# Gated DeltaNet scan in a hybrid encoder step: two 64-row inverses and a substitution in place of one 128-row inverse, in another order of work

## What is computed

```python
# gated delta rule; l tokens in a chunk; kb = k*beta
a_mat = where(strict, einsum('nbhid,nbhjd->nbhij', kb, kc) * decay, 0)
rhs = concatenate([vc * bc, kb * exp(gcum)], -1)
sol = triangular_solve(a_mat + eye(l), rhs, lower=True, unit_diagonal=True)
u, w = sol[..., :dv], sol[..., dv:]
qk = where(causal, einsum('nbhid,nbhjd->nbhij', qc, kc) * decay, 0)
def step(s, xs):                       # scan over the chunks
    v_new = u_i - w_i @ s
    o = (q_i * exp(g_i)) @ s + qk_i @ v_new
    s = s * exp(g_last) + (k_i * exp(g_last - g_i)).T @ v_new
```

## Time and profile before

| | |
|---|---|
| median of three runs | 1979.21 us (1976.8 to 1980.09) |
| profiled execution | 1982.12 us |
| its span, first to last instruction | 1980.4 us |
| PE, busy share of the span | 92% |
| PE weight loads | 87% |
| DVE, ACT, POOL | 41%, 26%, 31% |
| mean granted TensorE clock | 0.956 of full speed |
| chain that ended last, by engine | PE 75%, DVE 14%, ACT 4%, issue 4% |

### The profile page before, as it was taken

One profiled execution on the slowest core, in us unless ns is written; L12 is line 12 of the kernel. 1 busy time (PEld: TensorE's weight loads), 2 busy tenths in 40 slices (PEclk: granted clock), 3 DMA queues, 4 the chain that ended last, 5 costly groups with the idle time before them and its releaser, 6 DMA issues.

```text
span 1980.4 us, 29352 instructions
## 1 busy us (share of the span) xinstructions
PE 1826.4 (92%) x12590; PEld 1728.3 (87%) x12590; DVE 806.4 (41%) x1031; ACT 522.2 (26%) x987; POOL 620.3 (31%) x337
## 2 busy tenths in 40 slices
PE   4999999989998468887999999999999999999998
PEld 4989989977776258777899999999999999999898
DVE  5552125558996455656213322212222222225432
ACT  4222122337776233443213201010101010103211
POOL 4132223312340112123053434443444344332430
PEclk9999999999999578888799999999999999999999
DMA  5121322132003443342232111111111111111121
GB/s 166 44 71 39 108 66 76 55 118 67 1 1 107 105 102 94 89 107 53 52 93 75 43 53 44 43 43 54 43 43 43 54 43 43 43 53 61 51 61 46
DMA packets 197663, 126.50 MB, mean 64 GB/s; under 512 B 39024, under 2 KB 190980, under 8 KB 197540
## 3 DMA queue, kind: packets, MB, share of 16 engines
q1 hardware_dynamic: 188112, 111.69, 19.5%
q10 hardware_dynamic: 9428, 13.02, 1.8%
HBM read 100.07 MB, written 24.62 MB: 63 GB/s over the span
## 4 chain that ended last, share of the span: by engine, by line
PE 75%; DVE 14%; issue 4%; ACT 4%; DMA 2%; POOL 1%; SPq 0%; ACTq 0%; DVEq 0%; POOLq 0%
PE psum L2074 41%; PE psum L1892 8%; PE psum L2388 5%; PE psum L1861 3%; PE psum L1862 3%; PE psum L1863 3%; DVE act_lo_plain L1527 3%; PE psum L2207 2%; DVE act_hi_plain L1528 2%; DVE area L1630 1%; PE psum L2106 1%; PE psum L1944 1%; PE psum L2407 1%; DVE area L1467 1%; DVE act_lo L1764 1%
## 5 line engine op out<-in xcount | busy, mean ns | idle before, releaser
L2074 PE MATMUL psum<-act_hi,w_round 128*128 128x352 f32 x1920 | 369.8, 326 | 0.5 <-DVE act_lo L1764 0.5
L911 POOL TENSOR_TENSOR w_round<-w_plain,ones 128x1024 fp32r<-128x1024 f32 x80 | 173.8, 2173 | 533.1 <-DMA w_plain<-in_w_up_dram 231.2
L2074 PEld LDWEIGHTS psum<-act_hi,w_round 128*128 128x128 f32 x1920 | 321.8, 190 | 1.4 <-DVE act_lo L1764 0.8
L2074 PE MATMUL psum<-hid_hi,w_round 128*128 128x352 f32 x1344 | 260.0, 324 | 0.4 <-DVE hid_lo L1794 0.4
L2074 PEld LDWEIGHTS psum<-hid_hi,w_round 128*128 128x128 f32 x1344 | 224.9, 188 | 0.7 <-DVE hid_lo L1794 0.7
L1771 DVE TENSOR_TENSOR area<-psum,area 128x1056 f32<-128x1056 f32 x72 | 90.5, 1257 | 311.3 <-PE psum L2074 311.3
L2074 PE MATMUL psum<-act_lo,w_round 128*128 128x352 f32 x960 | 208.0, 325 | 0.0
L912 POOL TENSOR_TENSOR w_round<-w_plain,w_round 128x1024 fp32r<-128x1024 f32 x80 | 198.5, 2481 | 6.3
L1386 ACT ACTIVATE hid_hi<-area 128x1056 fp32r<-128x1056 f32 x28 | 30.4, 1088 | 592.5 <-DVE area L1787 592.5
L1861 PE MATMUL psum<-w_round,act_hi 128*128 128x256 f32 (+1 forms) x576 | 166.3, 289 | 6.6 <-POOLq L863 3.6
L2074 PEld LDWEIGHTS psum<-act_lo,w_round 128*128 128x128 f32 x960 | 164.4, 189 | 0.0
(11 more groups left out here) (294 smaller groups left out, 2911.0 us busy)
## 6 DMA issues: line engine op xcount, KB each, us to landing
w_plain<-in_w_up_dram SPq DMA_DIRECT2D x32, 512.0 KB, 4.1
w_plain<-in_w_down_dram SPq DMA_DIRECT2D x32, 512.0 KB, 3.4
w_plain<-in_w_in_dram SPq DMA_DIRECT2D x14, 1024.0 KB, 5.6
conv_scratch<-area ACTq DMA_DIRECT2D x12, 512.0 KB, 2.7
w_plain<-decay_scratch SPq DMA_DIRECT2D x9, 512.0 KB, 3.5
area<-t_scratch SPq DMA_DIRECT2D x9, 512.0 KB, 4.2
area<-x_scratch SPq DMA_DIRECT2D x9, 512.0 KB, 5.5
area<-in_x_prompt_dram SPq DMA_DIRECT2D x8, 512.0 KB, 3.2
```

The lines of the kernel that those rows point to most:

```text
L911: own.link(pool.tensor_tensor(hi, ring_raw(n), ones[:, 0:1].to_broadcast([P, RB]), ALU.mult))
L2074: last = pe.matmul(bank(bank_set(tile) + c)[:, 0:CH], w(k), a(k)[:, CH * c:CH * (c + 1)], start=(begins and k == ks[0] and w is w_h and a ...
```

## The change

The matrix of a chunk is treated as two halves of 64 rows. Only the two 64 by 64 inverses on the diagonal are made: both joins (16 to 32, 32 to 64 rows) are now products of 64 by 64 by 64 for each head and half (`block_products`, line 2206 of the new kernel), half 0 on rows and columns 0 to 63 of the array and half 1 on 64 to 127, in turns. The join to 128 rows, its copies and the second transposed product are gone. In its place the values are solved by substitution: `first_solved` multiplies both halves with their inverses, ACT copies the upper result (`upper_values`), `upper_on_lower` multiplies it with the off-diagonal block of `d_at`, ACT copies that (`lower_rest`), and `second_solved` adds its product with the lower inverse.

The scratch in DRAM and the transfers of `d_at`, `d_t` and `d_x` shrink to the two diagonal halves, each a transfer of its own. The loaded queries and keys, the norms, and the differences of the decays get a second buffer. The decays by key position for all heads (`d_gb`) and those for the own heads (`d_ge`) are loaded apart. `decayed_queries` goes from DVE to POOL and takes one instruction in place of two, as do `decayed_keys` and `decay_state` there. Banks are dealt out anew. The prompt's chunks go first, the sample's is last. The loops are now `for i in range(-1, CHUNKS + 1)`: the norms of chunks 0 and 1, the first decays and the first matrix are put between the steps of the sample's attention, and the joins of chunk i stand in the same step as its state's turn. SP's list is one loop over the chunks, and the loads for the output projection stand at its end.

```diff
+                if q < NT:
+                    for g in range(2):
+                        sp.dma_start(at_scratch[g], d_at[block_rows(g), q % 2, :, block_rows(g)]).then_inc(at_dumped, 16)
...
+                sp.wait_ge(at_dumped, 32 * q + (32 if q < NT else 16))
                 if q:
                     sp.wait_ge(scattered, 32 * q)
                 sp.dma_start(d_lane[:, 0:LB * LB].rearrange("l (r c) -> l r c", c=LB), at_lanes).then_inc(gathered, 16)
...
+            def matrices_in(q):
                 sp.wait_ge(scattered, 32 * (q + 1))
+                if q >= 2:
+                    sp.wait_ge(m_ready, steps(q - 2, 1))
+                for g in range(2):
+                    sp.dma_start(d_t[block_rows(g), q % 2], t_scratch[g]).then_inc(t_back, 16)
+                if q >= 2:
+                    sp.wait_ge(vn_ready, 2 * (q - 1))
+                for g in range(2):
+                    sp.dma_start(d_x[block_rows(g), q % 2], x_scratch[g]).then_inc(x_back, 16)
...
+            for q in range(CHUNKS):
+                blocks_out(q)
+                at(conv_qk_in, q + 2)
+                lanes_in(q)
+                at(own_sums_in, q + 1)
+                at(conv_v_in, q + 2)
...
+                    z_in(q - 2)
+                at(sums_in, q + 3)
+                lanes_out(q)
+                matrices_in(q)
+            sp.wait_ge(cn_made, CHUNKS)
+            ring_in(DN_RING)
+            sp.wait_ge(kv_turned, CHUNKS)
+            ring_in(DN_RING + 1)
+            z_in(NT - 1)
+            sp.wait_ge(m_ready, steps(NT, 0))
+            x_in_cols(0)
+            z_in(NT)
...
+            for i in range(-2, CHUNKS):
+                at(decay_state, i)
+                at(decayed_queries, i + 1)
+                at(decayed_keys, i + 1)
+                at(decays, i + 2)
...
+                    act.preload_act_table_set("natural_log_exp_and_others")
+                    act.wait_ge(g_stored, 16)
+                    act.wait_ge(consts_made, 6)
+                    logs(0)
...
+                if b == 3:
+                    squares(0)
+                if b == 5:
+                    squares(1)
+                if b == 6:
+                    inverse_norms(0)
+            decays(0)
...
             def second_masks(q):
-                act.wait_ge(m_ready, step_of(q, 1))
+                act.wait_ge(m_ready, steps(q, 1))
+                cols = slice(0, 2 * LB)
+                act.activation(d_m[:, :, cols], blocks(0, P)[:, :, cols], ACT.Copy,
+                               scale=level_rows[:, 2:3]).then_inc(m_made, 1)
...
+                    rows, cols = slice(HB * g, HB * g + 2 * LB), slice(2 * LB, HB)
+                    last = act.activation(d_x[rows, q % 2, :, cols], blocks(1, P)[rows, :, cols], ACT.Copy)
+                last.then_inc(x32_made, 1)
+            def upper_values(q):
+                act.wait_ge(vn_ready, 2 * q + 1)
+                act.activation(d_u[0:HB, :], bank(3)[0:HB, :], ACT.Copy).then_inc(u_made, 1)
+            def lower_rest(q):
+                act.wait_ge(a12_ready, q + 1)
+                act.activation(d_u[HB:P, :], bank(2)[HB:P, :], ACT.Copy).then_inc(u_made, 1)
...
+            for i in range(-1, CHUNKS + 1):
+                at(output_parts, i - 1)
+                if i >= 0:
+                    at(squares, i + 2)
+                at(turned_values, i + 1)
+                at(output_norms, i - 1)
+                prompt(second_masks, i)
+                at(logs, i + 2)
+                at(inverse_norms, i + 2)
+                prompt(second_blocks, i)
+                at(decays, i + 2)
+                prompt(upper_values, i)
+                prompt(lower_rest, i)
+                at(rounded_output, i - 1)
+                at(last_decays, i + 2)
+                at(state_decays, i + 2)
+                at(first_masks, i + 1)
...
+            for i in range(-1, CHUNKS + 1):
+                at(rest_of_values, i)
+                prompt(first_transposed, i)
+                at(lanes_begin, i + 1)
+                at(lanes_middle, i + 1)
+                at(first_blocks, i)
+                at(lanes_end, i + 1)
+                at(unit_norms, i + 2)
+                at(query_matrix, i + 1)
+                at(normed_output, i - 1)
+                at(key_matrix, i + 2)
+                at(new_values, i)
+                at(rest_of_output, i - 1)
+                at(decay_differences, i + 4)
+                at(new_state, i)
+                at(decayed_keys, i + 2)
+                at(output_squares, i)
...
                 pe.wait_ge(r_made, q + 1)
-                if q + 2 < CHUNKS:
-                    pe.wait_ge(at_made, q + 3)
+                if q < NT:
+                    pe.wait_ge(x32_made, q + 1)
...
                 for h in range(H):
                     cols = slice(HD * h, HD * (h + 1))
-                    last = pe.matmul(bank(5)[0:n, cols], d_x[0:n, q % 2, place_of(h), 0:n], d_r[0:n, cols],
+                    for g in range(2 if q < NT else 1):
+                        rows = block_rows(g) if q < NT else slice(0, n)
+                        last = pe.matmul(bank(3)[rows, cols], d_x[rows, q % 2, place_of(h), 0:min(n, HB)], d_r[rows, cols],
+                                         start=h == 0, stop=g == 0, skip_group_check=True)
...
+            def upper_on_lower(q):
+                pe.wait_ge(u_made, 2 * q + 1)
+                for h in range(H):
+                    cols = slice(HD * h, HD * (h + 1))
+                    last = pe.matmul(bank(2)[HB:P, cols], d_at[0:HB, q % 2, place_of(h), HB:P], d_u[0:HB, cols],
                                      start=True, stop=True)
+                last.then_inc(a12_ready, 1)
+            def second_solved(q):
+                pe.wait_ge(u_made, 2 * q + 2)
+                for h in range(H):
+                    cols = slice(HD * h, HD * (h + 1))
+                    last = pe.matmul(bank(3)[HB:P, cols], d_x[HB:P, q % 2, place_of(h), :], d_u[HB:P, cols],
+                                     start=False, stop=True, skip_group_check=True)
                 last.then_inc(vn_ready, 1)
             def state_change(q):
...
+            def block_products(b, q, left, right):
+                n = min(size(q), HB)
                 for h in range(H):
-                    last = pe.matmul(group(0, h, n), d_at[0:n, q % 2, place_of(h), 0:n],
-                                     d_t[0:n, q % 2, place_of(h), 0:n], start=True, stop=True)
+                    for g in range(2 if q < NT else 1):
+                        rows = slice(HB * g, HB * g + n)
+                        last = pe.matmul(bank(b)[rows, HB * place_of(h):HB * place_of(h) + n], left(h, g, rows, n),
+                                         right(h, g, rows, n), start=True, stop=True)
                 return last
...
+                if b == 7:
+                    square_sums(0)
+                turn_part(part_of(b))
+                part_values(part_of(b) - 1)
+            key_products(0)
+            part_values(2 * PARTS - 1)
+            turn_keys(0)
...
+            for i in range(-1, CHUNKS + 1):
+                at(keys_of_state, i)
+                prompt(first_transposed, i)
+                at(first_inverse, i)
+                prompt(second_matrices, i)
+                at(square_sums, i + 2)
+                prompt(second_inverse, i)
+                at(query_products, i + 1)
+                at(first_solved, i)
...
+                at(key_products, i + 2)
+                prompt(upper_on_lower, i)
+                at(turn_keys, i + 2)
+                prompt(second_solved, i)
+                at(turn_outputs, i - 1)
+                at(queries_of_state, i)
+                at(state_change, i)
+                at(first_matrices, i + 1)
+                at(outputs, i)
```

802 lines of the change are left out of this document (325 added, 477 removed).

## The result

The changed kernel takes **1864.0 us** (median of four runs, 1856.4 to 1870.2), the kernel before 1978.8; the ratio is 0.9419 (0.9377 to 0.9461). Forecast were 1883 and a range of 1855 to 1930: the direction and the places were right, and the gain of 115 us is a fifth above the 96 forecast.

What follows compares the result with a forecast made beforehand. PE, with waits, was taken to bound the middle step, 24.0 us for 34.7; 52 + 9 + 168 + 15 + 8 = 252 us for 348.1, a gain of 96, gave 1883 us, range 1855 to 1930.

Steps and rivals of the forecast that it cites:

- Price of the new groups: Middle step, joins and first solve: 1.38 us per 32 records, 8.3 for six groups, bounds 5.8 and 13.7.
- third rival: Middle step: quarters of the array don't overlap, clock mostly up; step 29.4 us, kernel 1921; chance 0.12.
- PE's sum: PE's work in a middle step after the change: 13.3 + 8.3 = 21.6 us, between 19.1 and 27.0.
- Waits: PE's waits in a middle step: 3.13 us ahead of the square sums gone, 1.4 us left in all.
- Slow clock: Middle step: 1 us added for PE's stretches at the 1.2 GHz level.
- The rule that I weighed and set aside: PE's clock: only idle gaps bring it down, so it would stay up; step 23 us, kernel 1876.
- The round of the lanes, first rival: Inverses' round through SP's queue: 21.6 us forecast; rival: 26.4 without slack, step 27, kernel 1904; chance 0.13.
- rival 5: A chunk's serial path of joins and substitution, 18 us, becomes the step; no chance of its own.
- Start: From the attention's end to the first `new_state`: 52 us in place of 77.1, bounds 45 to 60.
- Attention, last step, end: Attention 9 us longer (0 to 11); sample's last step 15 against 25.0 (10 to 25); end 8.0 as before.
- The cover for DVE: Middle step: DVE's work about 17.7 us, up to 6 more beside POOL's large instructions, just reaching 24.
- Second rival: Middle steps: groups near the lower bound, clock up, DVE holds at about 21 us; kernel 1862; chance 0.13.

Runs made afterwards that it cites:

- the late splitting: Changed kernel with POOL's splitting of the output projection's first weight block moved one step later; 1855.6 us, ratio 0.9393.
- the second profile: Profile of the changed kernel itself, run again without any edit as a yardstick; 1866.7 us, ratio 0.9441.

## Why the prediction was right, point by point

**Price of the new groups.** The bounds were 5.8 and 13.7 us for six; 8.3 was taken, and six groups of 1.10 to 1.15 us, two of them 2.08 together, are 6.6. The row taken as nearest (0.69 us for 16 records, L2181) was on the right side, for a reason only half right: either kind of alternation would have done. The third rival needed groups of 2.2 us; even without alternation they take 1.90. The lower bound was misread: its row, L2023 at 643.28, stands at a granted clock of 0.50. At 2.4 GHz the same form takes 0.65 us for 32 records, so the bound for six is 3.9 and not 5.8; the forecast didn't hang on it:

```profile
640.92 0.65 PE L2023 MATMUL psum<-w_plain,act_hi_plain 128*32 128x64 f32 x32
```

**PE's sum.** 21.6 forecast, 18.4 us busy. 1.7 of the difference is the groups. The rest is in the way of adding: the rows of the step sum to 20.0 us, since every row's duration reaches 0.07 us or more into the next, as the starts in PE's timeline show (722.16 + 1.10 is past 723.19), and over the step's rows this is 1.6 us.

**Waits.** 1.4 us forecast, 1.7 in the step shown (0.37, 0.57, 0.27, 0.49) and 1.3 to 3.0 in the first five. One of the four copies of ACT that were named as late next is among them (line 1310, at the second join). The waits that proved dear are others, for DVE's norms and for a load.

**Slow clock.** 1 us a step forecast; it was 0 in five steps and some 5 and 4 in two. That the sum came out near (9 for 7) is luck, the picture was wrong. I read the earlier trace rows as a fall with no long wait ahead of it. The wait of 1.25 us at 811.07 stands right ahead of that window, in the earlier trace rows, and a wait of 1.19 to 1.25 us recurs there in each of the six middle steps of before: in five of them PE has the lower clock within 3 us behind it, in one not. Two of them in PE's timeline of before, fallen and not:

```profile
813.47 1.98 PE L2112 MATMUL psum<-w_plain 64*128 64x128 f32 x16
```

```profile
881.57 1.11 PE L2112 MATMUL psum<-w_plain 64*128 64x128 f32 x16
```

In the profiles here most falls inside the steps stood behind waits of 1.06 to 3.3 us, while waits of 1.26 (changed kernel, 751.40) and 1.49 us (there, 810.51) brought none, and the fall at 843.8 us has none over 0.94 in the 5 us ahead of it. The rule that I weighed and set aside (the Trainium skill, TensorE: Matmul & The Clock Gate, "HAM oscillation — how this bites in real kernels": idle gaps bring the clock down) agrees with the late splitting's step better than my reading did. It is not the whole of it, as waits of equal length end either way, and one fall has only short ones ahead of it. What decides stays open.

**The round of the lanes, first rival.** The round was forecast at 21.6 us and is 21.7 from the first key matrix (653.1) to the first wait's end (674.8). (The terms as listed sum to 21.3; those of the serial path of rival 5 to 16.5, not 18. Neither moves the forecast.) The step of 24.0 gave it slack; at 20.8 there is none, and 3.4 us more cost 17, most of it through the clock. So this rival's mechanism is at work though its time (1904) is not: the step came down to the round, and that PE's sum alone bounds the step was wrong. The missing term was the issue: four loads and two stores of 0.65 us each stand in SP's queue between one chunk's blocks and the next.

**Start.** 52 forecast with bounds 45 to 60, measured 42.8, below the lower one; 46.2 in the second profile. The round was right but had no waits (1.4), the matrix came 1.5 us before the attention's end and not 2 behind (3.5), and the step that follows took 22.2 and not 27 (4.8).

**Attention, last step, end.** 9 and 9.0, which is luck in part, as the second profile has 6.1; 15 and 14.1; 8.0 and 7.2. The dense stage kept its time within 1.6.

**The cover for DVE.** DVE was to have 17.7 us of work, and POOL's large instructions up to 6 more. It has 17.2, and taking the queries back changed nothing. The interference was there, but it acts through PE's wait and the clock, not through DVE's sum. **Second rival** (1862, chance 0.13): this is what came, cheap groups and the clock mostly up, with a step near its 21 us, though the round sets that and not DVE's work alone. Its chance was set too low, since both of its halves hung on rows that I had taken for the wrong reason (L2152) or read too narrowly.

## What to carry to other kernels

Small matmuls on 64 by 64 tiles should alternate between tiles of the array, even where they are independent: the same work cost 0.75 us a group more in the plain order of loops. An earlier issue is not yet a shorter chain: measure the chain from end to end, as here 1.7 us of it came down to 0.9. Look also for the places where two engines meet by chance, since removing one such meeting and PE's wait of 2.4 us behind it gave 6 us in its step, the larger part through the clock. And when a clock's fall is read from a window, read also what stands ahead of the window's edge.

## What the runs showed of the hardware

- 32 records on 64 by 64 tiles take 1.15 us in turns on two quarters, 1.10 to 1.15 with only the rows or only the columns in turns, and 1.90 with eight products in one quarter after another; 16 records in one quarter 1.14.
- A copy of 64x256 on DVE took 1.97 us beside a 1.89 us instruction of POOL that had begun 0.15 us before it, 0.37 otherwise; a product of 128x1024 2.78 in place of 1.22. Where DVE began first, by 0.04 us, it took its 1.21 and POOL's 1.89 became 2.93.
- PE's clock fell behind single waits of 1.06 to 3.3 us and, at one place, behind three of 0.57 to 0.94 within 5 us, while single waits of 1.26 and 1.49 us brought no fall.
- The changed kernel's runs, with steps at 1.2 GHz in one profile that the other lacks, spread over 14 us (0.7%), where those of before, with such a stretch in every middle step, spread over 3.
